# Third block's norm and two projections in one program, and a tile-wise first unit for the HGRN output and query-key products

## What is computed

```python
y = (o * silu(gate)) @ w_out; x = x + gate1 * y        # first block, end of the HGRN mixer (w_out 2048 x 1024)
qk = silu(causal_conv(h @ w_in[:, 1024:2048], w, b))   # second block, mLSTM queries and keys, 4 taps
h = rms_norm_3(x, norm1_w) * (1.0 + scale1) + shift1   # third block
p = h @ w_in
pb = pb + (token_shift(pb) - pb) * mu                  # RWKV part, 14 blocks of 128 columns
qkv = silu(causal_depthwise_conv(qkv, conv_w))         # delta net part, 12 blocks of 128 columns, 4 taps
```

## Time and profile before

| what | value |
|---|---|
| time, median of 3 runs | 4342.48 us (4340.59 to 4346.35) |
| the profiled execution's own time | 4336.56 us |
| its span, first to last instruction | 4334.6 us |
| busy in the span: PE, DVE, ACT, POOL | 3856.6, 1874.0, 1302.3, 576.4 us |
| TensorE clock granted, mean | 0.933 of full |

### The profile page before, as it was taken

How to read it: one execution, slowest core, us unless ns; L and a number is a source line. 1 busy time by engine, 2 the same in 40 slices (tenths; PEclk the granted TensorE clock), 3 DMA queues, 4 the chain that set the end, 5 groups by cost and what they waited for, 6 DMA issues and landing times. The chain is left out here.

```text
span 4334.6 us, 59648 instructions
## 1 busy us (share of the span) xinstructions
PE 3856.6 (89%) x24539; PEld 2713.6 (63%) x24539; DVE 1874.0 (43%) x3047; ACT 1302.3 (30%) x2242; POOL 576.4 (13%) x302
## 2 busy tenths in 40 slices
PE   5899999997889998886999999999677768899998
PEld 2688888886634443344455546888537547687876
DVE  1455555555158883104213333533327446334431
ACT  1544444444222213023113323322331230423321
POOL 0000000000300000001000002444410010343442
PEclk7999999998999996987989999999889789999999
DMA  7211111110255544012311113332110100332332
GB/s 286 68 49 35 45 45 50 50 50 25 78 159 161 157 145 145 10 55 66 73 29 45 44 41 90 102 97 78 49 27 3 35 25 3 92 93 83 97 88 63
DMA packets 509892, 318.59 MB, mean 73 GB/s; under 512 B 28780, under 2 KB 491173, under 8 KB 509382
## 3 DMA queue, kind: packets, MB, share of 16 engines
q1 hardware_dynamic: 509638, 314.87, 24.8%
HBM read 310.64 MB, written 4.19 MB: 73 GB/s over the span
## 5 line engine op out<-in xcount | busy, mean ns | idle before, releaser
L1157 PE MATMUL cv_bank<-hT,cv_w 128*128 128x512 f32 x768 | 340.3, 598 | 14.2 <-DMA cv_w<-in_conv_w_in_dram 14.2
L1272 DVE SCALAR_TENSOR_TENSOR conv_u<-cv_pad,vec,conv_u 128x512 f32<-128x512 f32 x480 | 319.2, 743 | 0.0
L3018 POOL TENSOR_TENSOR tl_wl<-tl_w,tl_wh 128x1024 fp32r<-128x1024 f32 (+1 forms) x104 | 246.8, 2374 | 522.2 <-ACT tl_wh L3129 522.1
L1157 PEld LDWEIGHTS cv_bank<-hT,cv_w 128*128 128x128 f32 x768 | 144.9, 191 | 188.8 <-issue 173.7
L2070 POOL TENSOR_TENSOR mp_wl<-mp_w,mp_wh 128x1024 fp32r<-128x1024 f32 x72 | 173.6, 2413 | 596.3 <-ACT mp_wh L2150 596.3
L3129 ACT ACTIVATE tl_wh<-tl_w 128x1024 fp32r<-128x1024 f32 (+1 forms) x104 | 108.5, 1043 | 357.0 <-PE tl_bank L3055 354.4
L583 PE MATMUL hg_bank<-hg_hh,hg_wh 128*128 128x512 f32 x512 | 208.5, 407 | 0.0
L585 PE MATMUL hg_bank<-hg_hh,hg_wl 128*128 128x512 f32 x512 | 200.3, 391 | 0.0
L3053 PE MATMUL tl_bank<-tl_room,tl_wh 128*128 128x512 f32 x464 | 188.0, 405 | 13.3 <-POOL tl_wl L3018 12.5
L584 PE MATMUL hg_bank<-hg_hl,hg_wh 128*128 128x512 f32 x512 | 198.9, 389 | 0.0
L3055 PE MATMUL tl_bank<-tl_room,tl_wl 128*128 128x512 f32 x464 | 182.5, 393 | 0.0
(11 more groups left out here) (677 smaller groups left out, 8254.6 us busy)
## 6 DMA issues: line engine op xcount, KB each, us to landing
cv_ada<-in_w_ada_dram SPq DMA_DIRECT2D x48, 1024.0 KB, 7.5
hg_w<-in_hgrn_w_in_dram SPq DMA_DIRECT2D x80, 512.0 KB, 3.9
mp_w<-in_w_mlp_dram SPq DMA_DIRECT2D x64, 512.0 KB, 4.1
ada_w<-in_ada_w_dram SPq DMA_DIRECT2D x12, 2048.0 KB, 19.8
cv_w<-in_conv_w_in_dram SPq DMA_DIRECT2D x48, 512.0 KB, 4.0
tl_w<-in_w_ffn_in_dram SPq DMA_DIRECT2D x44, 512.0 KB, 3.9
at_w<-in_w_in_dram SPq DMA_DIRECT2D x24, 512.0 KB, 4.1
tl_w<-in_w_in_dram SPq DMA_DIRECT2D x20, 512.0 KB, 3.8
```

Source lines behind the costliest of these rows:

```text
L1157: ins = pe.matmul(ps[n % RING][:, :], W[n % SLOTS][:, k * P:(k + 1) * P], K.hT[:, k, :], start=(k == 0), stop=(k == KD - 1))
L1272: ins = dve.scalar_tensor_tensor(o, x, by, o, ALU.mult, ALU.add)
L3018: pool.tensor_tensor(WL[u % SPLIT][:, 0:n, :], W[u % RAW][:, 0:n, :], WH[u % SPLIT][:, 0:n, :].bitcast(F32), ALU.subtract).then_inc(low, 1)
```

## The change

`product_phase` and its helpers (`mat`, `tile_at`, `residual`, `act_into`), `conv4` and `shift_phase` are gone. `ho` and `qk` use `stream_phase`, written out without loops: PE starts on a unit 0 whose k-steps wait for one RL tile each, DVE makes the first WL, the RH tiles are split around the first WH, and six banks are used. `norm_phase` of the third block, `pb` and `gq` become one `front_phase` of 26 units with three WH/WL slots, in which the norm's tiles go straight into RH and RL; `gq` is so computed ahead of the RWKV phases and kept. POOL's masks move to `gates_phase`. Parts of RWKV's `bonus` lie in `pb`.

```diff
+def stream_phase(K, tag, w, x, kt, iters, col, on_act, on_dve, freed_by, start=None):
+    RAW, SPLIT, BANKS = 4 if kt <= KD else 2, 2, 6
+    AHEAD = kt // 2
...
+                for u in range(iters):
+                    wh, wl, bank = WH[u % SPLIT], WL[u % SPLIT], ps[u % BANKS]
+                    if u == 0:
+                        pe.wait_ge(low_first, 1)
+                    else:
+                        pe.wait_ge(low, u)
+                    if u >= BANKS:
+                        pe.wait_ge(freed, u - BANKS + 1)
+                    for k in range(kt):
+                        if u == 0:
+                            pe.wait_ge(r_low, k + 1)
+                        pe.matmul(bank[:, :], wh[:, k, :], RH[:, k, :], start=(k == 0), stop=False)
...
+                for k in range(kt):
+                    if k == AHEAD:
+                        weights_high(0)
+                    act.activation(RH[:, k, :], x[:, k, :], ACT.Copy).then_inc(r_high, 1)
+                for u in range(1, SPLIT):
+                    weights_high(u)
+                for u in range(iters):
+                    if on_act:
+                        act.wait_ge(summed, u + 1)
+                        on_act(act, u, ps[u % BANKS], freed, own)
+                    weights_high(u + SPLIT)
...
+                    if k == AHEAD:
+                        dve.wait_ge(high, 1)
+                        dve.tensor_tensor(WL[0][:, :, :], W[0][:, :, :], WH[0][:, :, :].bitcast(F32), ALU.subtract).then_inc(low_first, 1)
...
 def qk_phase(K, qk):
+        def on_act(act, i, bank, freed, own):
+            if i < 8:
+                if i >= 2:
+                    act.wait_ge(own[0], 4 * i - 4)
+                act.activation(pad[:, i % 2, 3:3 + T], bank[:, :], ACT.Copy).then_inc(freed, 1)
+            if i >= 1:
+                act.wait_ge(own[0], 4 * i)
+                act.activation(qk[:, i - 1, :], qk[:, i - 1, :], ACT.Silu).then_inc(own[1], 1)
...
+def front_phase(K, w_in3, pb, gq, RH, RL, t, sq):
+    RAW, SPLIT, BANKS, NB, NQ_ = 4, 3, 6, 14, 12
...
+                def after(u):
+                    act.wait_ge(summed, u + 1)
+                    if 2 <= u < NB + 2:
+                        act.wait_ge(shifted, u - 1)
+                    elif u >= 2:
+                        act.wait_ge(tap, 4 * (u - NB) - 4)
+                    act.activation(pad[:, u % 2, 3:3 + T], ps[u % BANKS][:, :], ACT.Copy).then_inc(padded, 1)
+                    if u > NB:
+                        gated(u - NB - 1)
...
+                weights_high(0)
+                weights_high(1)
+                act.wait_ge(sq_sum, KD)
+                act.activation(rstd[:, :], SUM[:, :], ACT.Ln, scale=1.0 / DM, bias=K.epsc[:, 0:1]).then_inc(ln_ok, 1)
...
+                for k in range(KD):
+                    act.activation(RH[:, k, :], t[:, k % 2, :], ACT.Identity, bias=shift).then_inc(h_high, 1)
+                    act.activation(K.hT[:, k, :], t[:, k % 2, :], ACT.Identity, bias=shift).then_inc(h_ok, 1)
+                    if k == 5:
+                        weights_high(2)
+                for u in range(1, NU):
+                    weights_high(u + SPLIT - 1)
+                    after(u - 1)
...
 def gates_phase(K, pb, lw, aa, gg, rows):
+            @block.gpsimd
+            def _(pool):
+                third_constants(K, pool, wide, made, fixed, masks)
...
+                dve.wait_ge(masks, 9)
                 dve.tensor_tensor_scan(rows[:, 1, :], K.keep64[0:8, :], r[:, 1, :], 0.0, ALU.mult, ALU.add).then_inc(rd, 1)
...
 def third_block(K):
-            norm_phase(K, [(K.xT, K.hT, T, K.at["g1_3"], M3, M3 + 8, 3)], third_constants)
-                shift_phase(K, w, pb)
+                front_phase(K, w, pb, gq, RH, RL, t, sq)
                 gates_phase(K, pb, lw, aa, gg, rows)
...
-                conv4(K, "gq", w, 0, 12, gq, K.at["gdn_w"], 12)
```

More of the change, by code:

```diff
@@ L868, in _ @@
                     recur(NH - 2 + p, p, 1 - p)
[L871 to L892, removed]
[L893 to L899 removed]
+def stream_phase(K, tag, w, x, kt, iters, col, on_act, on_dve, freed_by, start=None):
+    RAW, SPLIT, BANKS = 4 if kt <= KD else 2, 2, 6
+    AHEAD = kt // 2
+    w = w.rearrange("(k p) n -> p k n", p=P)
+    with ExitStack() as st:
+        W = [K.sb(st, f"{tag}_w{s}", [P, kt, P]) for s in range(RAW)]
+        WH = [K.sb(st, f"{tag}_wh{s}", [P, kt, P], F32R) for s in range(SPLIT)]
+        WL = [K.sb(st, f"{tag}_wl{s}", [P, kt, P], F32R) for s in range(SPLIT)]
+        RH = K.sb(st, f"{tag}_rh", [P, kt, T], F32R)
+        RL = K.sb(st, f"{tag}_rl", [P, kt, T], F32R)
         ps = K.psum_banks(st, tag)
         sems, old = K.phase()
[L902 to L903 removed]
+        w_in, (summed, freed, high, low_first, low, r_high, r_low), own = sems[0:RAW], sems[RAW:RAW + 7], sems[RAW + 7:]
         with K.nc.Block() as block:
@@ L907, in _ @@
                 clear_old(sp, old)
[L908 to L916, removed]
+                for u in range(iters):
+                    if u == RAW:
+                        sp.wait_ge(low_first, 1)
+                    elif u > RAW:
+                        sp.wait_ge(low, u - RAW)
+                    sp.dma_start(W[u % RAW][:, :, :], w[:, :, col + u * P:col + (u + 1) * P]).then_inc(w_in[u % RAW], 16)
@@ L918, in _ @@
             @block.gpsimd
             def _(pool):
[L920 to L927, removed]
+                for u in range(1, iters):
+                    pool.wait_ge(high, u + 1)
+                    pool.tensor_tensor(WL[u % SPLIT][:, :, :], W[u % RAW][:, :, :], WH[u % SPLIT][:, :, :].bitcast(F32),
+                                       ALU.subtract).then_inc(low, 1)
@@ L929, in _ @@
             @block.tensor
             def _(pe):
[L931 to L945, removed]
+                for u in range(iters):
[10 more added lines that the diff above has]
+                        pe.matmul(bank[:, :], wh[:, k, :], RH[:, k, :], start=(k == 0), stop=False)
+                        pe.matmul(bank[:, :], wh[:, k, :], RL[:, k, :], start=False, stop=False)
+                        ins = pe.matmul(bank[:, :], wl[:, k, :], RH[:, k, :], start=False, stop=(k == kt - 1))
+                    ins.then_inc(summed, 1)
@@ L947, in _ @@
             @block.scalar
             def _(act):
[L949 to L957, removed]
-                    ins.then_inc(high, 1)
@@ L1019 @@
+                if start:
+                    start(dve, own)
+                for u in range(iters):
+                    if freed_by == "dve":
+                        dve.wait_ge(summed, u + 1)
+                    else:
+                        dve.wait_ge(freed, u + 1)
+                    on_dve(dve, u, ps[u % BANKS], freed, own)
 CW, CP, GW = 31, 15, 64
```

257 lines of the change are left out of this document (148 added, 109 removed).

## The result

| | before | changed |
|---|---|---|
| median (lowest to highest), 4 runs each | 4341.53 us (4338.46 to 4346.35) | 4269.80 us (4265.80 to 4272.30) |
| ratio, 95% interval | | 0.9833 [0.9816, 0.9850] |
| the profiled execution's span | 4334.6 us | 4270.6 us |

A forecast was written before the change was run, and what follows sets the result against it. PE, busy 89% of the span, was taken as the bound, so gains come from its waits: 55.8 + 16.5 + 2.2 = 74.5 us, taken off the median, gives 4268.0 us; range 4256 to 4284.

The forecast's parts named there:

- Third block's front: Norm, `pb` and `gq` as one stage: from 224.2 to 168.4 us, a gain of 55.8 us, bounds 51 and 59.
- the pace: Front's 24 units behind the first two: 5.5 us each, taken between 5.44 and 5.57, 132.0 us in all.
- The held tile: Front's start: POOL's WL holds DVE's first scaled tile, moving it from 13.4 to 15.6 us; 2.2 us won if not held.
- Query and key products: Stage from 77.2 to 60.7 us, a gain of 16.5 us, between 13 and 18.5.
- The term of 2 us for held operations: Query and key products: DVE and POOL holding each other up plus one table load, 2 us for all units (0 to 5).
- rival 1: DVE and POOL become the bound in units with four taps; 11.6 us of gain stay away, 4280 us; chance 0.10.
- the port rule: GpSimd and two-input VectorE operations take one port pair in turn: four-tap units 5.86 us, 8.4 us lost in 20 units.
- HGRN output: PE starts 10.2 us after the first DMA issue, at 1106.3 instead of 1108.51: a gain of 2.2 us.
- The masks: POOL's 24.7 to 25.0 us of masks, costed at nothing in gates_phase, whose scan runs 41.3 us after the phase's start.
- 2 (straight code): About 1200 matmuls from code run once would lose 13 us to code arriving late, 4281 us; chance 0.06.
- 3 (clock): Lower clock granted in the front: 0.214 us more a matmul, up to 4402 us, slower than before; chance 0.02.
- 4: Front does not start early, as PE waits for the last RL tile: 12 us go, 4280 us; chance 0.02.

The follow-up runs named there:

- the skipped bytes: Changed kernel with unused bytes a partition ahead of the front's weight tiles: 224 bytes 4271.1 us, 0.2267 us a matmul; 32 bytes 4273.2 us, 0.2333.

## Why the prediction was right

- **Third block's front.** Start of PE 17.8 forecast, 17.45 measured; units 0 and 1 done at 31.4, measured 31.5; end behind the last unit 5.0, measured 4.6. The mis-sized term is the pace: 5.5 us a unit taken between 5.44 and 5.57, 5.60 measured, outside both. That is 24 x 0.1 = 2.4 us, of which the shorter end gave 0.4 back: a miss of 2.1. The forecast gave the two paces to two stretches without a cause; the skipped bytes show that they belong to the places of the tiles. What one phase instead of three gives by itself, with one start and one end less of the products, was not tried.
- **The held tile.** The hold was taken as in tail_phase and was there, on the second tile instead of the first; with WL on DVE the 2.0 us came back. The Trainium skill (SBUF — State Buffer, SBUF: two separate sides) has the pair locked for the whole instruction: the 3.50 against 1.41 us agree with it.
- **Query and key products.** 60.7 forecast, 59.9 measured. The term of 2 us for held operations was 0.9: PE waited once, 0.6 us for the WL behind the table load in front of the first Silu. That unit began 6.21 us behind the one before and the next 5.58 behind it; all others behind the first took 5.43 to 5.46. The taps alone take 0.55 + 2.33 = 2.9 us without the loop's gaps, not 3.5, so with WL's 2.4 they are 5.3, under a unit. This is why rival 1 did not come, in the form that the port rule gave it as well: a tap was held (2.77 us instead of 0.75, beside a WL of 2.87), and PE did not see it. The reason given for the gain, the Silu off the chain, was half of it; the 9.3 us of the other half are mostly a clock that was no longer lost in pauses. The forecast had them in its number all the same, since it counted the new stage at the full pace.
- **HGRN output.** 2.2 forecast, 3.0 measured; PE 10.2 us behind the issue, measured 10.35. From the stage's start PE came 2.4 us sooner, and its first unit, less of it at the lower clock, took 0.4 less. The weights had not landed, and the copy waited for them, as assumed. WL took 2.29 us at 2048 elements. The Trainium skill's (VectorE: DVE Perf Modes, The TRN2 errata) formula gives the same 2.29.
- **The masks** cost nothing in gates_phase (the scan 39.9 us after its start, 41 forecast), and would have cost 14 us in the front.
- **The rivals.** 2 (straight code) is refuted for the pace: the same code ran at 0.2267 once its tiles stood elsewhere. 3 (clock): 0.96 in the front. 4: PE started early, and without that 11.2 us would be gone, 12 in the forecast.
- **The sum.** 74.0 us in the three stages against 74.5. That it is so close is in part luck: the front missed by -2.1 us, the other two by +0.8 each. The span of the profile missed by 10.5 us (4260.1 against 4270.6) since the unchanged stages took longer in that execution; the medians show 71.7.

## What to carry to other kernels

Where an engine finishes one unit and prepares the next in one stream, put the part that waits for another engine one unit later; a further slot hides that wait from PE, but not from the engine's own round, which then comes out at the end. Look at what a pause does beyond its length: here the clock fell with pauses of 3 us and stayed with pauses of 1 to 2.3. And compare the pace of a matmul between stages: up to three per cent hung on where two tiles started, at no instruction's cost.

## What was not expected of the hardware

- The pace of a 128x512 matmul at full clock took values from 0.2267 to 0.2333 us by the places of weights and activations, each the same from unit to unit over hundreds of matmuls.
- POOL and DVE delay each other in more than subtractions: a TENSOR_SCALAR took 2.24 us instead of 0.55 beside a WL, and POOL's masks took 28.6 us beside DVE's scaled tiles and RL, 25.0 beside the scaled tiles alone and 23.2 beside next to nothing.
- The front's norm reached its root 11.6 to 11.7 us after the stage's start in six executions and 12.8 to 12.9 in six, the same code among both. The clock splits them the same way: it rose to full 5.0 to 5.3 us after the stage's start in the first six and 7.9 us after it in the others.
- gates_phase took 52.1 to 53.1 us in the executions in which the lower clock was granted for 14 to 19 us of it, 54.5 to 54.7 at 24 us and 56.5 to 57.4 at 30 to 31 us, with the same instructions on PE. What decides when the clock moves there, these runs don't tell. Effects of 2 to 4 us were therefore read from their stage, not from the total.
